# Reordering the last chunk's attention around three groups of expert dots in layer 1

## The reference

```
x = x + g_a * (softmax(q k^T / sqrt(128)) v) @ w_o
h = modulate(rmsnorm(x, norm_ffn), sh_f, sc_f)
x = x + g_f * peer_ffn(h)
```

## Time and profile before

| what | value |
|---|---|
| median of three runs | 2339.73 us |
| the profiled execution's own time | 2342.71 us |
| its span in the profile | 2340.9 us |
| TensorE busy | 1645.7 us, 70% |
| VectorE busy | 1549.1 us, 66% |
| ScalarE busy | 875.2 us, 37% |
| GpSimd busy | 954.5 us, 41% |
| DMA | 927.92 MB, mean 396 GB/s |
| expert fetches (line 736) | 764 |
| dots (line 2412) | 764, 1227 ns each |

### The profile page before, as it was taken

How to read it: one execution, slowest core, us unless ns; L and a number is a source line. 1 busy time by engine, 2 the same in 40 slices (tenths; PEclk the granted TensorE clock), 3 DMA queues, 4 the chain that set the end, 5 groups by cost and what they waited for, 6 DMA issues and landing times.

```text
span 2340.9 us, 27431 instructions
## 1 busy us (share of the span) xinstructions
PE 1645.7 (70%) x9193; PEld 721.9 (31%) x9193; DVE 1549.1 (66%) x3640; ACT 875.2 (37%) x2596; POOL 954.5 (41%) x840
## 2 busy tenths in 40 slices
PE   7998887767876666767555766678787755555556
PEld 3655543323333222323211222225453311111111
DVE  1227667887767667877767676653867877766654
ACT  2223443345443233443333444442523333332323
POOL 1113344535454444444444454430344545444441
PEclk9999998889898888878777887888998977776788
DMA  9998899999999999999999999994699999999997
GB/s 399 381 365 344 346 397 419 420 421 414 420 414 420 420 420 416 418 413 416 409 419 408 422 421 419 418 371 182 265 377 418 419 421 421 422 421 422 421 421 299
DMA packets 140490, 927.92 MB, mean 396 GB/s; under 512 B 17063, under 2 KB 24007, under 8 KB 33342
## 3 DMA queue, kind: packets, MB, share of 16 engines
q0 software_dynamic: 112816, 807.16, 83.7%
q1 hardware_dynamic: 27390, 119.01, 12.8%
q10 hardware_dynamic: 144, 0.01, 0.0%
HBM read 924.97 MB, written 1.15 MB: 396 GB/s over the span
## 4 chain that ended last, share of the span: by engine, by line
DMA 44%; PE 28%; DVE 16%; issue 5%; ACT 4%; POOL 2%; SPq 0%; POOLq 0%; DVEq 0%; ACTq 0%
DMA arena<-in_uv,small 42%; PE bank L1465 12%; DVE arena L2412 8%; PE bank L797 3%; PE bank L762 2%; ACT aux L1728 2%; POOL arena L736 2%; PE bank L153 1%; DMA arena<-in_ada 1%; PE bank L1121 1%; PE bank L944 1%; PE bank L783 1%; DVE aux L2334 1%; ACT small L1721 1%; PE bank L774 1%
## 5 line engine op out<-in xcount | busy, mean ns | idle before, releaser
L736 POOL DMA_INDIRECT arena<-in_uv,small x764 | 907.1, 1187 | 1170.7 <-PE bank L1465 880.0
L1465 PE MATMUL bank<-arena,aux 64*64 64x512 f32 x5888 | 916.6, 767 | 613.8 <-ACT aux L1728 576.7
L2412 DVE CUSTOM_DVE_ANT_0 arena<-arena,h 128x1024 f32<-128x1024 f32 x764 | 920.1, 1227 | 453.0 <-DMA arena<-in_uv,small 428.3
L1465 PEld LDWEIGHTS bank<-arena,aux 64*64 64x64 f32 x5888 | 258.8, 171 | 1204.0 <-ACT aux L1728 691.2
L1721 ACT ACTIVATE small<-small 128x4 f32<-128x4 f32 (+3 forms) x212 | 43.5, 205 | 1095.0 <-DVE small L2412 1085.1
L1728 ACT ACTIVATE aux<-aux,small 128x64 f32<-128x64 f32 x768 | 206.4, 336 | 7.0 <-ACT small L1721 0.2
L1703 ACT ACTIVATE aux<-small 128x64 f32<-128x64 f32 x768 | 204.4, 336 | 11.6 <-issue 2.6
L797 PE MATMUL bank<-hT,aux 128*128 128x256 f32 (+1 forms) x752 | 162.9, 372 | 4.6 <-ACT hT L1534 2.4
L797 PEld LDWEIGHTS bank<-hT,aux 128*128 128x128 f32 x752 | 133.1, 195 | 47.7 <-issue 26.0
L1675 ACT ACT_TABLE_LOAD x73 | 93.7, 1283 | 1.3
L148 POOL DMA_DIRECT2D mod_rows<-aux x24 | 12.4, 521 | 124.2 <-DVE aux L2200 73.4
(11 more groups left out here) (318 smaller groups left out, 1657.4 us busy)
## 6 DMA issues: line engine op xcount, KB each, us to landing
arena<-in_ada SPq DMA_DIRECT2D x36, 1024.0 KB, 10.1
aux<-in_w_query SPq DMA_DIRECT2D x43, 512.0 KB, 8.1
arena<-in_uv,small POOLq DMA_INDIRECT x764
arena<-in_w_head SPq DMA_DIRECT2D x16, 512.0 KB, 10.4
hT<-in_ada SPq DMA_DIRECT2D x7, 1024.0 KB, 9.2
arena<-in_w_qkv SPq DMA_DIRECT2D x3, 2048.0 KB, 20.7
h<-in_ada SPq DMA_DIRECT2D x5, 1024.0 KB, 13.3
arena<-in_w_o SPq DMA_DIRECT2D x4, 1024.0 KB, 10.4
```

Of the source, the lines that this page charges most:

```text
L736: nc.gpsimd.indirect_dma_start(out=slot_at(pos), out_offset=None, in_=d["uv"][unit // FIRST], in_offset=bass.IndirectOffsetOnAxis(ap=self. ...
L1465: last = nc.tensor.matmul(bank[2 * r + m][out:out + 64, :], self.dg[rr, (s + o) % 8, :], slot_at(at)[rr, cols], start=first, stop=False)
L2412: last = nc.vector.tensor_tensor_reduce(out=slot_at(at)[:, 0:D], in0=slot_at(at)[:, 0:D], in1=h[:, c * D:(c + 1) * D], scale=1.0, scalar=0 ...
```

## The change

In the attention's steps, VectorE takes unit 32's first group of dots at u = 2, its second at u = 4, and its third in two halves at u = 6 and 7. Unit 33's best sixteen move from u = 2 to u = 3, the first stage of its choice from u = 4 to u = 5, and the rest of the choice goes behind step 5. ScalarE does the first group at u = 2 (after the copy of the last turned queries and the output copy of head 1, which is taken out of step 3), the second at u = 4, and unit 33's gates at u = 6. TensorE does head 1's value product at step 3 ahead of head 2's transposes, the first `combine` and the wait for unit 33's tops at u = 4, the second `combine` at u = 5; the first three heads of `late_out(0)` stay at u = 7. Behind the attention TensorE goes to the third `combine` at once, where before it did heads 3 and 4 of `late_out(0)` first; all five remaining heads follow in one piece.

```diff
                         if 1 <= u <= H:
                             g_transposes(first + u - 1)
-                        if 2 <= u < H + 2:
+                        if 2 <= u < H + 2 and u != 3:
                             g_values(first + u - 2)
...
+                    def second_values():
+                        g_values(H + 1)
+
                     def first_group():
                         pe.wait_ge(o_copied, last_count(2 * H, H + 1))
                         combine(FIRST, 0)
+                        tops_taken()
 
                     def second_group():
+                        combine(FIRST, 1)
+
+                    def first_heads():
                         late_out(0, 0, 3)
-                        combine(FIRST, 1)
-
-                    g_attention(H, {0: next_score, 2: lambda: turned_transposes(7), 4: first_group, 5: tops_taken, 7: second_group})
-                    late_out(0, 3, 5)
+
+                    g_attention(H, {0: next_score, 2: lambda: turned_transposes(7), 3: second_values, 4: first_group, 5: second_group, 7: first_heads})
                     combine(FIRST, 2)
-                    late_out(0, 5, H)
+                    late_out(0, 3, H)
                     late_out(1)
                     combine(FIRST, 3)
...
-                        if u >= 2:
+                        if u >= 2 and u != 3:
                             g_out_copies(first + u - 2)
...
                     def first_group():
+                        turned_copies(7)
+                        g_out_copies(H + 1)
                         gated_identities(FIRST, 0)
                         group(FIRST, 0)
 
-                    g_attention(H, {2: lambda: turned_copies(7), 3: first_group, 5: lambda: gates(FIRST + 1, False), 6: lambda: group(FIRST, 1)})
+                    g_attention(H, {2: first_group, 4: lambda: group(FIRST, 1), 6: lambda: gates(FIRST + 1, False)})
                     group(FIRST, 2)
...
-                    g_attention(H, {0: lambda: raw_scale(7), 1: half_turned, 2: next_tops, 3: lambda: dots(FIRST, 0, range(GRP)),
-                                    4: lambda: choose(FIRST + 1, 1), 5: lambda: dots(FIRST, 1, (0, 1)), 6: lambda: dots(FIRST, 1, (2, 3))},
-                                {4: rest_chosen})
-                    dots(FIRST, 2, range(GRP))
+                    g_attention(H, {0: lambda: raw_scale(7), 1: half_turned, 2: lambda: dots(FIRST, 0, range(GRP)), 3: next_tops,
+                                    4: lambda: dots(FIRST, 1, range(GRP)), 5: lambda: choose(FIRST + 1, 1),
+                                    6: lambda: dots(FIRST, 2, (0, 1)), 7: lambda: dots(FIRST, 2, (2, 3))},
+                                {5: rest_chosen})
                     dots(FIRST, 3, range(GRP))
                     finish_gates(FIRST + 1)
```

## The result

The changed kernel takes 2344.87 us (median of 17 runs, 2338.64 to 2347.1), the kernel before beside it 2340.26 (17 runs, 2337.8 to 2344.88): ratio 1.0014, 95% interval 1.0007 to 1.002, or 3.3 us (1.6 to 4.7). The change is inside 0.2% and slightly slower: no gain. The profiled execution's own time is 2345.04, its span 2343.3. Between the two kernels' traces the first fetch of unit 32, which stands ahead of everything that the change touches, has moved from 1647.39 to 1648.53; these 1.14 us (the shift) are taken off where times of the two traces are compared.

What follows compares the result with a forecast made beforehand. The end of late_out(1), on a chain of TensorE and VectorE, was taken to set the total; +0.6 - 1.1 + 1.8 + 0.8 = +2.1 us on 2339.73 gave 2341.8 us, range 2336.5 to 2345.5.

Steps and rivals of the forecast that it cites:

- The bound: The end of late_out(1) decides the total, through the last gated fetch at 1728.16; gaps ahead count only if that moves.
- Attention on VectorE: Third group's dots add 4.57 us, 3.62 us idle goes; with 0.3 us of waits, head 7's scaling ends 0.6 us later.
- the upper bound: +4.7 us at late_out(1)'s end: 1.5 of waits, 1.7 for a clock fall at the third combine, 0.5 at the second.
- Transposes at once: On TensorE head 7's transposes follow its scaling at once, where they started 1.1 us behind it: -1.1 us.
- The pause's start and end: Third combine still starts 3.62 us behind head 7's values, near 1697; a ScalarE drain would add an estimated 1.4 us.
- Two heads behind the combine: Heads 3 and 4 of late_out(0) lose the cover of ScalarE's table load on TensorE: +1.8 us.
- The clock: TensorE's clock may fall in the 2.5 us pause ahead of the third combine, adding 1.7 us; half, 0.8, was taken.
- The sum: +0.6 - 1.1 + 1.8 + 0.8 = +2.1 us at late_out(1)'s end and at the run's end.
- the likeliest case: Closed DMA gaps are given back at later gates: +1.0 to +4.7 us, 2340.7 to 2344.4; chance 0.80.
- Rival 1: Gaps stay closed because the gates at 1700 and 1711 don't bind: up to 8.5 us won, 2331.2; chance 0.06.
- Rival 2: VectorE's first dots wait for their fetched slots, delaying the attention: slower by over 4.7 us; chance 0.14.
- The DMA's idle stretch: With all sixteen slots in by 1692, DMA idles about 9 us until 1702, another 2 or 3 ahead of late_out's gate.

Runs made afterwards that it cites:

- e5: Kernel before with 18 unread identity matmuls on TensorE ahead of late_out(1): median 2345.96 us against 2341.01, ratio 1.0016.
- e8: Kernel before, unchanged, a single execution for a second trace; late_out(1) ends 64.21 us behind the start of unit 32's first fetch.
- e1: Changed kernel with heads 3 and 4 of late_out(0) put back ahead of the third combine: median 2340.45 us, ratio 1.0000 to the kernel before.
- e4: Changed kernel with 14 unread identity matmuls in TensorE's pause ahead of the third combine: median 2341.73 us, ratio 1.0006 to the kernel before.
- e6: Changed kernel with late_out(0)'s head 3 at u = 7 and heads 4 and 5 ahead of the third combine: median 2339.3 us, ratio 0.9991.
- e7: Changed kernel with late_out(0)'s head 3 and ScalarE's third group at u = 7, third combine at u = 9: 2339.94 us, ratio 0.9997.
- e3: Changed kernel with both edits, e1's and e2's: median 2339.93 us, ratio 0.9999 to the kernel before.
- e2: Changed kernel with VectorE's third group of dots back behind the attention: 2342.33 us, ratio 1.0005 to the kernel before.

## Why the prediction was right, and where its sum was off

**The bound.** Right: the gaps among unit 32's fetches are not what sets the end. They closed (share 0.67 to 0.98), and the end came later, by about what `late_out(1)` was late. e5 shows that link by itself, without the change. The 2.4 us of L against 3.3 of F fit it less well with the first trace of before; with the second F is +2.3 and L +2.2. That the gate of F is the last that the stream meets was not so in the trace it was read from: unit 34's first fetch, at 1746.50, was held up there too (e8). It hangs on the same chain, so the forecast didn't suffer.

**Attention on VectorE.** Expected first combine near 1666, measured 1667.40, less the shift 1666.26; second 1676.4, measured 1676.50; scaling of head 7 at +0.6, measured +0.88 (1692.73 - 1.14 = 1691.59 against 1690.71). The waits are 0.19 + 0.44 = 0.63 us where 0.3 was taken, one for an Exp and one for head 6's scores. The latter is the row of TensorE named for the upper bound: the second combine's clock fell (5.36 us behind 3.79 of pause), at 0.44 of the 0.5 us that the bound had for it. The middle of the sum had nothing for this fall.

**Transposes at once.** -1.1 expected; head 7's values now 1693.73, before 1693.99: -0.26 in all, of which -1.14 is this term.

**The pause's start and end.** Expected third combine near 1697, measured 1698.49 - 1.14 = 1697.35. The Gelu starts 1.29 us behind its load again, so no drain stands there in this trace either, and the 1.4 us that a drain by the Trainium skill (ScalarE: Activation LUTs, What ACT_TABLE_LOAD costs) would have added did not come.

**Two heads behind the combine.** +1.8 expected, 11.43 - 9.71 = +1.72 measured; e1 gives it back.

**The clock.** This is the term that was mis-sized. The pause was named as 2.5 us and is 2.49, but half of the fall's price was taken, 0.8, for want of a reason to decide. It fell in full: 5.36 - 3.66 = 1.70, and e4 shows that the pause is what brought it down at this place. Of the ten traces eight have the third combine at 3.66 or 3.67 behind a pause under 1 us or none, and two at 5.36 and 6.48, both behind 2.49. The nearest row, the first combine of before (pause 2.50 us, 5.36), would have given the right price. But the length of the pause doesn't settle it. Behind 2.58 us the first combine of the changed kernel ran at full clock, as did those of e1, e4, e6 and e7 behind 2.50, with the transposes and scores of a head between pause and combine; behind the 2.44 us ahead of L757 the clock fell in nine of ten traces, behind the same pause in e6 it didn't. And in the trace of before it had been down, and up again, just ahead of that first combine (L1308 at 1664.88 took 1.92 us for eight records, 1.06 at full clock). So 1.7 was the better choice, not a certain one. The rule of the Trainium skill (TensorE: Matmul & The Clock Gate, Part 1), that the array is throttled by default and activity releases it, agrees with the third combine, and by it the sum was 3.0; applied to every pause of some 2.5 us it would be wrong for the 2.58.

**The sum.** 0.88 - 1.14 + 1.70 + 1.72 = +3.16 us at M; +2.1 was expected. From the second trace of before it is +2.47. The timed runs say +3.3 (1.6 to 4.7); on the median that the prediction started from, 2339.73, that is 2343.0, 1.2 above the forecast. The rest of the 3.1 us between 2341.8 and 2344.87 can be the spread of runs: before itself had medians of 2339.73, 2340.26, 2340.29 and 2341.01. So the mechanism was right and the size low, and it took some luck that the number held: 2344.87 lies above the 2344.4 of the likeliest case, and inside the range to 2345.5 only by the 1.3 us added for the scatter of runs.

**The rivals.** Rival 1 is refuted: the third combine comes no earlier than worked out, and the gates at 1702.66 and 1716.02 bind. No kernel here came near its 8.5 us: even e6 and e7, with M 1.2 to 2.3 us ahead of before, gain 2.1 us (0.0 to 4.2) and 0.7 (-1.4 to 2.8). Rival 2 is refuted: VectorE waits for no fetch in the first group. The DMA's idle stretch that was expected for 1692 to 1702 lies in 1695 to 1704, the one ahead of `late_out`'s gate in 1715 to 1719.

**Open.** Why t0 differs by 9.5 us between executions, and why the clock falls behind a pause in one trace and not, or not yet, in another: the eight records of L757, all behind 2.43 or 2.44 us, took 1.97 us in e3, 1.89 in e7, 1.49 in e5 and 1.09 in the seven others. With what follows in L797, that moves F against M by up to 2.9 us (15.84 in e6, 18.74 in e5), nearly as much as the change itself. What e2's edit alone is worth is known to about 2 us only.

## What to carry to other kernels

Before closing a gap in a stream, find the last gate that still has idle DMA beside it: here the gaps ahead of it were worth nothing, and work put in front of it cost its whole length. A lead at that gate pays only as far as there is idle DMA to fill (e6). Work that TensorE does while it would wait for another engine is free and can keep its clock up; taken from there it cost both here, 1.7 + 1.7 us. And when a row of the trace shows nearly the situation that the change makes, start from its whole price, then look for rows with the same pause and another outcome: they say how far to trust it.

## What the runs showed of the hardware that was not expected

The clock's fall is not the same in every execution of one program, and the length of the pause ahead doesn't set it: the first combine of before took 5.36 us in one trace and 6.10 in another, with pauses of 2.50 and 3.90 us ahead. Behind the same 3.79 us the second combine took 5.36 in the changed kernel and four others, 6.44 in e3 and 6.55 in e2. An fp32 matmul of a 128x128 identity shows as two records: 14 of them 3.29 us, 18 of them 4.18. The start of the same fetch, behind 1640 us of the same program, lay anywhere from 1641.45 to 1650.99 in ten traces, more than any of these edits moved the run; only times measured from it could be compared.
